# Modulation units of the first MLP taken up earlier, their columns read before the fourth up-slab, and the third sum's adding DMA issued ahead of one load

## The reference, cut to what is touched

```python
    c_act = jax.nn.silu(c)
    for i in range(DEPTH):
        mod = c_act @ ada_w[i] + ada_b[i]
        sh1, sc1, g1, sh2, sc2, g2 = jnp.split(mod, 6, axis=-1)
        ...
        h = modulate(rmsnorm(x, norm_mlp_g[i]), sh2, sc2)
        x = x + g2[:, None, :] * sq_relu_mlp(h, mlp_w1[i], mlp_w2[i])

def sq_relu_mlp(h, w1, w2):
    return jnp.square(jax.nn.relu(h @ w1)) @ w2
```

## Time and profile before

| | us |
|---|---|
| runs | 1770.12, 1771.18, 1766.01 |
| median | 1770.12 |
| profiled execution, whole | 1770.68 |
| its span, from the first to the last instruction | 1769.4 |
| TensorE busy (share of the span) | 1723.8 (97%) |
| VectorE busy | 1225.5 (69%) |
| ScalarE busy | 755.0 (43%) |
| GpSimd busy | 126.0 (7%) |
| mean granted TensorE clock | 0.992 of full |

### The profile page before, as it was taken

How to read it: one execution, slowest core, us unless ns; L and a number is a source line. 1 busy time by engine, 2 the same in 40 slices (tenths; PEclk the granted TensorE clock), 3 DMA queues, 4 the chain that set the end, 5 groups by cost and what they waited for, 6 DMA issues and landing times. The chain is left out here.

```text
span 1769.4 us, 22801 instructions
## 1 busy us (share of the span) xinstructions
PE 1723.8 (97%) x9273; PEld 1396.4 (79%) x9273; DVE 1225.5 (69%) x1418; ACT 755.0 (43%) x922; POOL 126.0 (7%) x131
## 2 busy tenths in 40 slices
PE   7999999999999999999999999999999999999997
PEld 4488777888788788888888786777888888888886
DVE  4688767866885565757447767775668578578579
ACT  4353434343332353535345623453544344344344
POOL 0101010001100000000000011110000000000002
PEclk9999999999999999999999999999999999999999
DMA  9967464745631446454312232003344434336324
GB/s 369 409 210 220 145 198 131 236 143 191 224 130 52 148 104 197 116 146 143 119 48 78 79 95 69 5 2 120 119 119 116 146 96 143 123 92 181 105 72 131
DMA packets 141673, 246.43 MB, mean 139 GB/s; under 512 B 15118, under 2 KB 50598, under 8 KB 141313
## 3 DMA queue, kind: packets, MB, share of 16 engines
q1 hardware_dynamic: 122432, 192.76, 32.1%
q0 software_dynamic: 18992, 51.62, 12.0%
q10 hardware_dynamic: 144, 0.59, 0.1%
HBM read 239.69 MB, written 6.83 MB: 139 GB/s over the span
## 5 line engine op out<-in xcount | busy, mean ns | idle before, releaser
L2156 DVE TENSOR_TENSOR w_lo<-raw,w_hi 128x2048 fp32r<-128x2048 f32 x99 | 227.5, 2298 | 161.2 <-ACT w_hi L1567 160.8
L1567 ACT ACTIVATE w_hi<-raw 128x2048 fp32r<-128x2048 f32 x103 | 197.2, 1915 | 280.5 <-PE bank L756 176.7
L756 PE MATMUL bank<-h_hi,w_hi 128*128 128x512 f32 x736 | 291.6, 396 | 4.6 <-DVE h_lo L2203 2.9
L756 PE MATMUL bank<-h_hi,w_lo 128*128 128x512 f32 x736 | 287.1, 390 | 0.0
L756 PE MATMUL bank<-h_lo,w_hi 128*128 128x512 f32 x736 | 287.1, 390 | 0.0
L756 PE MATMUL bank<-f_hi,w_hi 128*128 128x512 f32 x496 | 193.0, 389 | 0.0
L756 PE MATMUL bank<-f_lo,w_hi 128*128 128x512 f32 x496 | 193.0, 389 | 0.0
L756 PE MATMUL bank<-f_hi,w_lo 128*128 128x512 f32 x496 | 192.9, 389 | 0.0
L756 PEld LDWEIGHTS bank<-h_hi,w_hi 128*128 128x128 f32 x736 | 138.6, 188 | 38.0 <-issue 7.4
L756 PEld LDWEIGHTS bank<-h_hi,w_lo 128*128 128x128 f32 x736 | 138.4, 188 | 29.3
L756 PEld LDWEIGHTS bank<-h_lo,w_hi 128*128 128x128 f32 x736 | 138.7, 188 | 28.2 <-issue 0.5
(11 more groups left out here) (452 smaller groups left out, 3062.9 us busy)
## 6 DMA issues: line engine op xcount, KB each, us to landing
raw<-in_mlp_w SPq DMA_DIRECT2D x82, 512.0 KB, 5.1
ada_ring<-in_ada_w SPq DMA_DIRECT2D x12, 2048.0 KB, 15.2
ada_ring<-in_ada_w POOLq DMA_DIRECT2D x16, 1024.0 KB, 5.9
raw_more_mlp<-in_mlp_w SPq DMA_DIRECT2D x32, 512.0 KB, 4.7
raw<-in_w_ffn_up SPq DMA_DIRECT2D x32, 512.0 KB, 4.9
raw_more_ffn<-in_w_ffn_up SPq DMA_DIRECT2D x32, 512.0 KB, 4.8
xT<-in_mlp_w SPq DMA_DIRECT2D x26, 512.0 KB, 5.6
raw<-in_w_in SPq DMA_DIRECT2D x20, 512.0 KB, 4.6
```

The source lines that it names most:

```text
L756: mm = te.matmul(bank[:, b + n], x, y, start=first and k == 0 and j == 0, stop=last and k == 3 and j == 2, skip_group_check=s == SLABS["ff ...
L1567: se.activation(m.ring(s)[0], m.raw_place(s), ACT.Copy).then_inc(sem("hi_made"), 1)
L2156: ve.tensor_tensor(lo, m.raw_place(s), hi.bitcast(F32), ALU.subtract).then_inc(sem("lo_made"), 1)
```

## The change

Three things, all in the first MLP.

- The table gives (1, 0) and (2, 0) two units instead of one, and (1, 3) and (2, 3) none. The numbers of units in a quarter stay the same; the third quarter's entries are not changed.
- VectorE reads the columns right after the sum s4, ahead of the block work that follows it, and reads those of the units up to (q, 1) instead of up to (q, 2). TensorE makes no column sums after the fourth up-slab of q = 0, 1 and 2; the unit of (q, 2) is summed after the first up-slab of the next quarter, as the fourth unit was before.
- GpSimd issues the addition for s3 before, not after, the last of the two loads that stood ahead of it.

```diff
-ADA1_UNITS = {(1, 0): 1, (1, 1): 1, (1, 2): 1, (1, 3): 1, (2, 0): 1, (2, 1): 1, (2, 2): 1, (2, 3): 1,
+ADA1_UNITS = {(1, 0): 2, (1, 1): 1, (1, 2): 1, (2, 0): 2, (2, 1): 1, (2, 2): 1,
               (3, 0): 2, (3, 1): 1, (3, 2): 1, (3, 3): 1, (3, 4): 1, (3, 5): 1, (3, 6): 1}
@@ TensorE, mlp
         plain = QUARTERS[stage]
+        read_before = [stage_slab(stage, q, 3) for q in range(plain)]
...
                     ada_sums(11)
-                ada1_sum(ada1_units(s - 1))
+                if s not in read_before:
+                    ada1_sum(ada1_units(s - 1))
@@ VectorE, mlp
                 if q < plain and g:
                     s4(stage, q)
+                    if layer == 0 and q:
+                        ada1_mod(ada1_units(stage_slab(stage, q - 1, 1)), ada1_units(stage_slab(stage, q, 1)))
                     t3(stage, q, 0)
...
             if q < plain:
-                if layer == 0 and q:
-                    ada1_mod(ada1_units(stage_slab(stage, q - 1, 2)), ada1_units(stage_slab(stage, q, 2)))
                 products_lo(stage, q)
...
-    ada1_mod(ada1_units(stage_slab("mlp0", 2, 2)), ADA1_IN_MLP)
+    ada1_mod(ada1_units(stage_slab("mlp0", 2, 1)), ADA1_IN_MLP)
@@ GpSimd
         add("mlp0", q, "s1", 1, 1)
-        loads(4 * q - 1, 4 * q + 2)
+        loads(4 * q - 1, 4 * q + 1)
         add("mlp0", q, "s3", 1, 0)
+        loads(4 * q + 1, 4 * q + 2)
```

## The result

| | before | after |
|---|---|---|
| median, first comparison | 1769.61 us (6 runs) | 1760.80 us (6 runs) |
| ratio, with its 95% interval | | 0.9948 (0.9938 to 0.9958) |
| median, the same kernel in a later comparison | 1769.54 us (14 runs) | 1763.17 us (5 runs) |
| ratio, with its 95% interval | | 0.9963 (0.9950 to 0.9976) |
| profiled execution, span | 1770.68, 1769.4 us | 1762.02, 1760.7 us |

The account below looks back on a forecast made before the run. TensorE, busy 1723.8 of 1769.4 us, was taken as the bound; removing losses of 8.12 us in q = 1 and 2.43 in q = 2, 10.55 in all, gave 1760 us, range 1756.5 to 1766.

Parts of the forecast that it names:

- The units: VectorE, up-slab 0: the moved modulation unit takes 3.96 of 4.68 us idle, 0.7 to spare; cost nothing.
- The split of s1: VectorE splits s1's weights from about 208.6 to 210.9, s1 ready 0.9 us early; gain 1.77 us in q = 1.
- The load of s3: SP's load of s3 to GpSimd's adding DMA: 5.50 us instead of 8.84, as nothing runs beside it; bounds 5.50 to 8.84.
- the neighbour: GpSimd's 1 MB modulation load, issued at 211.64 beside SP's load of s3, taken as why that step took 8.84 us.
- The addition: Adding DMA for s3 takes 11.75 to 12.88 us; ScalarE starts at 228.3 to 229.4, so s3's 3.26 us go.
- The load behind the addition: 1 MB modulation load right behind s3's addition on GpSimd's queue: delay taken as 0, bounds 0 to 5.9 us.
- the rival "slower": Load following s3's addition delays it by up to 5.9 us; s3 late again, kernel 5.8 us slower, 1776; chance 7%.
- The half clock: TensorE after s3's wait in q = 1: 3.09 us lost at the 1.2 GHz level, to go with the wait.
- the sum of 10.55 us: Total forecast gain from a11's end to the next up-slab: 8.12 us in q = 1 plus 2.43 in q = 2.
- If the waits are gone and the time has moved by less than 8 us, something later gave it back: Sign for the changed kernel's trace: TensorE's waits gone but under 8 us moved means a later loss.
- the 4.34 us of the prediction: Time from ScalarE's start on s3 at 234.66 to TensorE's start of s3 at 239.00, in q = 1.

Follow-up runs that it names:

- the table alone: Kernel before with only the new table of units, column read and GpSimd's order left as they were; ratio 0.9958 (0.9943 to 0.9972) against the kernel before.
- the order alone: Kernel before with only the addition for s3 issued ahead of the last load on GpSimd; ratio 0.9987 (0.9977 to 0.9998) against the kernel before.
- The second profile: Kernel before, unchanged, profiled again; the seven products of q = 1 and q = 2 took 44.12 and 40.24 us; ratio 1.0001 (0.9991 to 1.0011).
- the column read alone: Kernel before with only the columns read early (TensorE's sums placed to match), old table and load order; ratio 1.0006 (0.9993 to 1.0019) against the kernel before.

## Why the prediction held, step by step

- *The units.* Right. The two units of up-slab 0 leave VectorE 0.77 us idle ahead of the split at 174.49 (0.7 forecast), and unit 2 starts at 176.70 straight behind it, so its load was there.
- *The split of s1.* Right. It runs from 208.81 to 211.10 (208.6 to 210.9 forecast) and waits for ScalarE; TensorE takes s1 at 211.82, 0.72 us after the split (1.17 by the forecast's 210.9 and 212.07). The column read at 203.22 costs nothing; the runs show that moving it gains some 0.15 us a quarter at most.
- *The load of s3.* The 5.50 us are right (5.40), the reason is only half so. It was put down to the neighbour; a neighbour that starts 0.23 us later does no harm to this step. It was the head start of 1.97 us. And the new order on GpSimd, from which the prediction took the 5.50, was not needed for it: the table alone moves the load 12 us forward and gives 5.59 us, as the order alone does.
- *The addition.* Right: 11.88 us (11.75 to 12.88), ScalarE at 228.44 (228.3 to 229.4), TensorE at s3 at 233.62 without a wait. That SP's load went out 2.45 us sooner was listed as help for s3; by itself it gives 0.33, since TensorE comes to s3 sooner by nearly as much: 233.62 - 211.16 = 22.46 us from load to need after, 235.51 + 0.23 - 213.61 = 22.13 before.
- *The load behind the addition*, the one unknown: 0 was taken, and the addition takes 11.88 us with it and 11.90 without. The kernel after shows the reason, in the view of DMA issues from 209 to 226 us and in GpSimd's queue from 227 to 233 us:

```profile
xT<-in_mlp_w POOLq DMA_DIRECT2D x2, 512.0 KB, 9.8
ada_ring<-in_ada_w POOLq DMA_DIRECT2D x1, 1024.0 KB, 14.4
```
```profile
q0 software_dynamic: 325, 1.12, 49.7%
```

  The load lands 14.4 us after its issue instead of 5.9, at 232.4. Its 1 MB moves from about 227 us on, when the addition is nearly through; from 221.56 to 227 the queue moved 0.97 MB, the addition's. So the rival "slower" fell. The prediction's own reason for the 0, that an addition yields little to a neighbour, does not hold: in these runs it took 10.84 to 13.04 us. The rule of the Trainium skill behind it (page "DMA: Bandwidth & Descriptors", section "Issuing engines are not separate DMA queues": transfers interleave on the same 16 engines, whoever issued them) holds in these traces between two queues, where a load 0.23 us behind s3's is stretched to 7.6 us; behind an addition on one queue the trace shows no such cost.
- *The half clock*, 3.09 us. The mechanism was right, the size was that of one execution. The second profile lost 44.12 - 38.09 - 1.68 - 2.36 = 1.99 us to it, with 1.68 and 2.36 the lost steps at s1 and s3. This is the mis-sized term: the sum of 10.55 us was made wholly from an execution whose wait at s3 and clock were worse than in the second one. So 1760.0 stands beside the first median of 1760.8, and 3.2 us below the second of 1763.2. That the first came so near is luck in part: the mean spans of the runs whose span is recorded, 61 before and 11 after, are 1767.9 and 1760.1 us, 7.8 apart, where the forecast had 10.
- *"If the waits are gone and the time has moved by less than 8 us, something later gave it back"* was the wrong alternative for the second comparison with its 6.4 us: part was given back later, by falls of the clock that nothing ties to the change, and part had not been there to gain.

## What to carry to other kernels

A wait's name is its last releaser: before moving that instruction, ask what made it late; here a multiply-add unit two rows ahead, and moving the named read alone gained nothing. Look at what a large load starts just ahead of: in this kernel 1 MB cost the critical load most with a head start of 2 us, and nothing when it started 12 us ahead or behind the dependent DMA on the same queue. Before the sum is made from one profiled execution, separate the terms that every execution has (waits) from those that vary (a clock that falls behind a wait), and give the latter a range down to nothing.

## What the hardware showed that was not expected

- The same wait can end with or without a fall of the clock. With the column read alone TensorE waited 2.03 us ahead of s1 in both quarters; in q = 1 the clock then fell, in q = 2 it stayed at 1.00 (columns as above):

```profile
213.00:216.00 3.00, 2.66 (x8) 2.13 (x9) 2.78 (x3) 0.84 (x2) 0.00 (x0) 0.67 0.93 332
216.00:219.00 3.00, 3.00 (x12) 2.40 (x11) 2.67 (x4) 0.00 (x0) 0.00 (x0) 0.76 0.83 248
...
301.00:304.00 3.00, 2.90 (x13) 2.42 (x14) 2.90 (x3) 0.59 (x2) 0.00 (x0) 1.00 0.91 328
```

- In that kernel s3 did not wait in q = 1, although its chain (19.28 us) was longer than in the kernel after. TensorE, slowed behind s1, came to it at 236.87; at full clock it would have come at about 213.34 + 96 x 0.2267 = 235.1, and s3 was ready at 232.48 + 4.34 = 236.82 (both estimates, from the pace of q = 0 and the 4.34 us of the prediction). Here a fall of the clock hid the next wait.
